# A one-core kernel of two blocks: recurrent merges ahead of the spatial gate, context turns and router shares later, positions added by GpSimd, and three projections in three passes

## What is computed

```python
xn = rms_norm(x, norm_g)
z = xn @ w_in                       # qa ka va fa ga | xb gb | qc kcc ... gc | ud vd gd | mg
y_a = fox_attention(...)            # 8 heads, forgetting attention
y_b = rg_lru(xb, ...)               # recurrent branch
y_c = nsa_attention(...)            # compressed, selected and window attention
u, v = gelu(ud), layer_norm(gelu(vd), ln_v_g)
y_d = u * (einsum('gts,bcsgd->bctgd', w_spatial * causal, v) + b_spatial)
ys = stack([y_a * silu(ga), y_b * silu(gb), y_c * silu(gc), y_d * silu(gd)])
proj = einsum('bsnw,nwd->bsnd', ys, w_branch)          # 4 branches, 512 -> 1024
merged = sum(sigmoid(mg) * proj, axis=branches)
x = x + merged @ w_out
```

## Time and profile before

| | |
|---|---|
| time, median of 3 | 1083.97 us (1081.85 to 1086.04) |
| the profiled execution, its own time | 1090.9 us |
| its span in the trace | 1088.8 us |
| mean granted TensorE clock | 0.955 of full speed |
| TensorE matmul busy | 1007.3 us, 93% |
| VectorE busy | 612.8 us, 56% |
| ScalarE busy | 441.5 us, 41% |
| GpSimd busy | 49.5 us, 5% |

### The profile page before, as it was taken

How to read it: one execution, slowest core, us unless ns; L and a number is a source line. 1 busy time by engine, 2 the same in 40 slices (tenths; PEclk the granted TensorE clock), 3 DMA queues, 4 the chain that set the end, 5 groups by cost and what they waited for, 6 DMA issues and landing times.

```text
span 1088.8 us, 13871 instructions
## 1 busy us (share of the span) xinstructions
PE 1007.3 (93%) x5638; PEld 764.9 (70%) x5638; DVE 612.8 (56%) x1065; ACT 441.5 (41%) x709; POOL 49.5 (5%) x66
## 2 busy tenths in 40 slices
PE   7999989999997998898979999995989999999984
PEld 5688667775896988678967886895965753566521
DVE  4777736563655455326574898666842511597605
ACT  4356532954664443124464101335632300556401
POOL 2000000000000000000010222000000000000010
PEclk8999989999998999899989999997899999999987
DMA  9634676765424744624322134002978997999993
GB/s 302 201 135 148 218 267 232 255 224 206 167 78 155 260 166 155 232 86 156 109 95 92 53 141 155 1 1 68 398 292 303 350 382 284 399 404 404 407 350 142
DMA packets 110413, 230.66 MB, mean 212 GB/s; under 512 B 8300, under 2 KB 15757, under 8 KB 110350
## 3 DMA queue, kind: packets, MB, share of 16 engines
q1 hardware_dynamic: 104144, 216.44, 54.8%
q0 software_dynamic: 2880, 9.71, 2.3%
q10 hardware_dynamic: 3326, 3.63, 1.1%
HBM read 221.11 MB, written 8.65 MB: 211 GB/s over the span
## 4 chain that ended last, share of the span: by engine, by line
PE 75%; DVE 14%; DMA 6%; ACT 3%; issue 2%; ACTq 0%; DVEq 0%
PE bank L791 9%; PE bank L1532 7%; PE bank L1533 7%; PE bank L1534 7%; PE bank L2595 6%; PE bank L756 5%; PE bank L2534 4%; PE bank L2535 4%; PE bank L2536 4%; PE bank L2619 3%; DMA more_slots<-in_moe_w_up 2%; PE bank L1446 2%; PE bank L2527 2%; PE bank L1575 2%; PE bank L967 1%
## 5 line engine op out<-in xcount | busy, mean ns | idle before, releaser
L1532 PE MATMUL bank<-rounded 128*128 128x256 f32 (+1 forms) x656 | 201.8, 308 | 9.0 <-DVE slot_rounded L680 4.3
L1533 PE MATMUL bank<-rounded 128*128 128x256 f32 x592 | 168.4, 284 | 0.0
L1532 PEld LDWEIGHTS bank<-rounded 128*128 128x128 f32 x656 | 126.3, 192 | 21.2 <-issue 9.7
L1534 PE MATMUL bank<-rounded,slot_rounded 128*128 128x256 f32 x472 | 134.8, 286 | 0.0
L791 PE MATMUL bank<-x_and_h,slot 128*128 128x256 f32 x544 | 129.1, 394 | 4.9 <-ACT x_and_h L595 4.9
L791 PEld LDWEIGHTS bank<-x_and_h,slot 128*128 128x128 f32 x544 | 106.1, 198 | 22.4 <-issue 7.7
L1533 PEld LDWEIGHTS bank<-rounded 128*128 128x128 f32 x592 | 113.9, 192 | 1.2 <-issue 1.0
L1522 DVE TENSOR_TENSOR slot_rounded<-slot,rounded 128x1024 fp32r<-128x1024 f32 (+1 forms) x63 | 67.1, 1086 | 68.9 <-ACT rounded L1516 68.7
L1534 PEld LDWEIGHTS bank<-rounded,slot_rounded 128*128 128x128 f32 x472 | 91.3, 193 | 0.0
L839 ACT ACTIVATE arena<-bank 128x256 f32<-128x256 f32 x56 | 21.4, 384 | 118.0 <-PE bank L791 96.3
L1516 ACT ACTIVATE rounded<-slot 128x1024 fp32r<-128x1024 f32 (+1 forms) x63 | 57.7, 943 | 27.0 <-PE bank L1534 23.3
(11 more groups left out here) (493 smaller groups left out, 2067.4 us busy)
## 6 DMA issues: line engine op xcount, KB each, us to landing
slot<-in_w_in SPq DMA_DIRECT2D x26, 2048.0 KB, 8.0
slot<-in_ada_w SPq DMA_DIRECT2D x12, 2048.0 KB, 8.4
slot<-in_moe_w_down SPq DMA_DIRECT2D x11, 2048.0 KB, 16.1
...
```

The source lines that it names most:

```text
L1532: t.do.matmul(dst, w_hi, x_hi, start=start, stop=False)
L1533: t.do.matmul(dst, w_hi, x_lo, start=False, stop=False)
L1534: return t.do.matmul(dst, w_lo, x_hi, start=False, stop=stop)
```

## The change

1. `placed` moves from VectorE to GpSimd, with the same operands and waits; it can run as soon as the positions have landed and h1 is made.
2. `FIRST_PIECES` gets 12 more pieces: gb, ud (4 `channels` each) and vd (4 `pieces`, where there were two `tokens` jobs). They are done in three passes from the h1 of the merges; splits are written two pieces ahead, beginning in gc 2 and gc 3. A weight's first use counts from the job that writes its split. The homes are shared with the query/key tiles, so their splits wait for `head_norm` and `heads` of qc and for the last mixing of forgetting attention.
3. `h1_split` moves from behind `spatial_norm` to behind `cmp_keys`; `spatial_mask` is split off and stands before `cmp_keys`; `spatial_norm` takes one epsilon and one root for both tiles, and Newton steps and scales move to `spatial_scale`, ahead of merge 1 1.
4. In `PLAN` the merges of branch 1 move ahead of gd and `spatial`; `merge_start` 3 stands behind spatial 3. The costs of the fill change (vd counts four `pieces`), so the weave shifts from the first pieces on.
5. The context's turns stand one to five jobs later than their scans; the router's nine share instructions stand behind the one-hot rows 0 and 1.

The core of the diff (`tensor_pieces` takes its parts of h1 from `parts_of_h1` in the same way, and the `pieces` and `channels` functions of ScalarE and VectorE write the split that `piece_beside` names):

```diff
+        SQ0, SQ1 = SQ_HOME, SQ_HOME + NT * W
+        FIRST_HOMES += [Y3, SQ0, SQ1, Y3] + [SQ0, V_HOME, Y3, SQ0] + [V_HOME, Y3, SQ0, V_HOME]
...
-                           ("xb", ("channels", "xb", 3)), ("ud", ("channels", "ud", 3)), ("vd", ("tokens", "vd", 1))):
+                           ("xb", ("channels", "xb", 3)), ("ud", ("channels", "ud", 3)), ("vd", ("pieces", "vd", 3))):
...
+        LATER_FIRST = len(FIRST_PIECES)
+        FIRST_PIECES += [*channels("gb"), *channels("ud"), *in_pieces("vd")]
+
+        def piece_beside(job):
+
+            if job in channels("gc")[2:]:
+                return LATER_FIRST + job[2] - 2
+            p = FIRST_PIECES.index(job) + 2 if job in FIRST_PIECES else len(FIRST_PIECES)
+            return p if p not in (LATER_FIRST, LATER_FIRST + 1) and p < len(FIRST_PIECES) else None
...
-        spatial = [*ud[2:], *tokens("vd"), ("spatial_norm",), *channels("gd"), *[("spatial", j) for j in range(WT)]]
+        spatial = [*ud[2:], *in_pieces("vd"), ("spatial_norm",)]
+        gated = [*channels("gd"), *[("spatial", j) for j in range(WT)]]
         ada = [job for c in range(13) for job in ((("ada", c),) if c < 12 else ()) + ((("ada_turn", c - 1),) if c else ())]
         merge = {n: [("merge", n, dt) for dt in range(KT)] for n in range(4)}
 
-        fill, scored = spread(early + lru + spatial, ada, 10) + merge[1], attention(UNITS)
+        fill, scored = spread(early + lru + spatial, ada, 10) + merge[1] + gated, attention(UNITS)
...
-        PLAN += woven([*channels("cf0"), ("ctx_scan", 0), ("ctx_turn", 0, 0), ("ctx_turn", 0, 1),
-                       *channels("cf1"), ("ctx_scan", 1), ("ctx_turn", 1, 0), ("ctx_turn", 1, 1), *tokens("cv"),
+        PLAN += woven([*channels("cf0"), ("ctx_scan", 0), ("channels", "cf1", 0), ("ctx_turn", 0, 0), ("channels", "cf1", 1),
+                       ("ctx_turn", 0, 1), *channels("cf1")[2:], ("ctx_scan", 1), ("tokens", "cv", 0), ("ctx_turn", 1, 0), ("tokens", "cv", 1), ("ctx_turn", 1, 1),
...
-        PLAN.insert(PLAN.index(("spatial_norm",)) + 1, ("h1_split",))
+        PLAN.insert(PLAN.index(("cmp_keys",)) + 1, ("h1_split",))
         for n in range(4):
-            before = {3: ("merge", 1, KT - 1), 0: ("merge", 3, KT - 1), 2: ("merge", 0, KT - 1)}.get(n, ("merge", n, 0))
+            before = {3: PLAN[PLAN.index(("spatial", WT - 1)) + 1], 0: ("merge", 3, KT - 1), 2: ("merge", 0, KT - 1)}.get(n, ("merge", n, 0))
             PLAN.insert(PLAN.index(before), ("merge_start", n))
+        PLAN.insert(PLAN.index(("cmp_keys",)), ("spatial_mask",))
+        PLAN.insert(PLAN.index(("merge", 1, 1)), ("spatial_scale",))
...
-            for name in names:
+            for name in (*names, *([FIRST_PIECES[piece_beside(job)][1]] if piece_beside(job) else [])):
...
-        @part(VECTOR, "placed")
-        def vector_placed(v):
-            v.wait_ge(*at("position_in"))
-            v.wait_ge(*now("h1"))
-            v.do.tensor_tensor(xT[:, :, :], xT[:, :, :], merged, ALU.add).then_inc(*inc("x_placed"))
+        @part(GPSIMD, "placed")
+        def gpsimd_placed(g):
+            g.wait_ge(*at("position_in"))
+            g.wait_ge(*at("h1", KT - 1))
+            g.do.tensor_tensor(xT[:, :, :], xT[:, :, :], merged, ALU.add).then_inc(*inc("x_placed"))
...
+        def parts_of_h1(p):
+
+            if p < LATER_FIRST:
+                return first_high_of_h1, first_low_of_h1, ("split_first_low", 1)
+            return h1_high, h1_low, ("split_h1_low", 1)
...
-            if p >= 3:
-                a.wait_ge(*at(*FIRST_PIECES[p - 3]))
+            held = [o for o in range(p) if FIRST_HOMES[o] == FIRST_HOMES[p]]
+            if held:
+                a.wait_ge(*at(*FIRST_PIECES[held[-1]]))
             if FIRST_HOMES[p] in (M0, M1):
                 a.wait_ge(*at("x_placed"))
+            if FIRST_HOMES[p] == SQ0:
+                a.wait_ge(*at("head_norm", "done", "qc"))
+            if FIRST_HOMES[p] == SQ1:
+                a.wait_ge(*at("heads", "qc", 1))
+            if p >= LATER_FIRST and FIRST_HOMES[p] == V_HOME:
+                a.wait_ge(*at("mixed", UNITS[2 * WT - 1]))
...
-                high, _, low = first_piece(FIRST_PIECES.index(job))
-                t.wait_ge(*at("split_piece_low", FIRST_PIECES.index(job)))
+                p = FIRST_PIECES.index(job)
+                high, _, low = first_piece(p)
+                h_high, h_low, h_done = parts_of_h1(p)
+                t.wait_ge(*at(*h_done))
+                t.wait_ge(*at("split_piece_low", p))
                 for k in range(KT):
-                    mm = three_passes(t, bank[:, 0:S], high[:, k, :], low[:, k, :], first_high_of_h1[:, k, :], first_low_of_h1[:, k, :], k == 0, k == KT - 1)
+                    mm = three_passes(t, bank[:, 0:S], high[:, k, :], low[:, k, :], h_high[:, k, :], h_low[:, k, :], k == 0, k == KT - 1)
...
+        @part(VECTOR, "spatial_mask")
+        def vector_spatial_mask(v):
+            v.wait_ge(*at("spatial_in"))
+            v.do.tensor_tensor(wsT, wsT, bcast(causal_T, 1, 8), ALU.mult).then_inc(*inc("spatial_norm"))
+
         @part(VECTOR, "spatial_norm")
         def vector_spatial_norm(v):
-            v.wait_ge(*at("spatial_in"))
-            v.do.tensor_tensor(wsT, wsT, bcast(causal_T, 1, 8), ALU.mult).then_inc(*inc("spatial_norm"))
             for tt in range(NT):
                 stats, mv = bn[:, tt, 0:6], bn[:, tt, 6:8]
                 v.wait_ge(*at("tokens_out", "vd", tt))
                 v.do.bn_stats(stats, vd[:, tt, :]).then_inc(*inc("spatial_norm"))
                 v.wait_ge(*now("spatial_norm"))
                 v.do.bn_aggr(mv, stats).then_inc(*inc("spatial_norm"))
-                v.wait_ge(*now("spatial_norm"))
-                v.do.tensor_scalar(bn[:, tt, 8:9], bn[:, tt, 7:8], EPS, None, ALU.add).then_inc(*inc("spatial_norm", "var", tt))
+            v.wait_ge(*now("spatial_norm"))
+            v.do.tensor_scalar(bn[:, :, 8], bn[:, :, 7], EPS, None, ALU.add).then_inc(*inc("spatial_norm", "var"))
+
+        @part(SCALAR, "spatial_norm")
+        def scalar_spatial_norm(a):
+            a.wait_ge(*at("spatial_norm", "var"))
+            scalar_root(a, "spatial_norm", (), bn[:, :, 8], bn[:, :, 9])
+
+        @part(VECTOR, "spatial_scale")
+        def vector_spatial_scale(v):
+            v.wait_ge(*at("root", "spatial_norm"))
+            vector_newton(v, "spatial_norm", bn[:, :, 8], bn[:, :, 9], bn[:, :, 10])
             for tt in range(NT):
-                v.wait_ge(*now("spatial_norm"))
-                v.wait_ge(*at("root", "spatial_norm", tt))
-                vector_newton(v, "spatial_norm", bn[:, tt, 8:9], bn[:, tt, 9:10], bn[:, tt, 10:11])
...
-            for which, oh in enumerate((oh1, oh2)):
-                v.do.tensor_tensor(tmp16, oh, prob, ALU.mult).then_inc(*inc("router_steps"))
-                v.wait_ge(*now("router_steps"))
-                v.do.tensor_reduce(share[:, which], tmp16, AX_X, ALU.add).then_inc(*inc("router_steps"))
-                v.wait_ge(*now("router_steps"))
-            v.do.tensor_tensor(total, share[:, 0], share[:, 1], ALU.add).then_inc(*inc("router_steps"))
-            v.wait_ge(*now("router_steps"))
-            v.do.reciprocal(total, total).then_inc(*inc("router_steps"))
-            v.wait_ge(*now("router_steps"))
-            v.do.tensor_tensor(share, share, bcast(total, 1, 2), ALU.mult).then_inc(*inc("router", "shares"))
...
             onehot(0)
             onehot(1)
+
+
+            for which, oh in enumerate((oh1, oh2)):
+                v.do.tensor_tensor((tmp16, pick)[which], oh, prob, ALU.mult).then_inc(*inc("router_steps"))
+                v.wait_ge(*now("router_steps"))
+                v.do.tensor_reduce(share[:, which], (tmp16, pick)[which], AX_X, ALU.add).then_inc(*inc("router_steps"))
+                v.wait_ge(*now("router_steps"))
+            v.do.tensor_tensor(total, share[:, 0], share[:, 1], ALU.add).then_inc(*inc("router_steps"))
+            v.wait_ge(*now("router_steps"))
+            v.do.reciprocal(total, total).then_inc(*inc("router_steps"))
+            v.wait_ge(*now("router_steps"))
+            v.do.tensor_tensor(share, share, bcast(total, 1, 2), ALU.mult).then_inc(*inc("router", "shares"))
```

40 lines of the change are left out of this document (20 added, 20 removed).

## The result

The changed kernel takes 1075.24 us, median of 6 runs (1072.13 to 1076.46), against 1084.33 us for the kernel before in the same session (6 runs). The ratio is 0.9898 with a 95% interval of 0.9872 to 0.9924: 11 us faster (8 to 14; the medians alone are 9 apart), where 22 had been forecast. The time lies just inside the range (1048 to 1076), the size of the gain does not fit. The profiled execution of the changed kernel took 1076.5 us, 1.2 over its median; that of the kernel before took 1090.9, 6.9 over the median of its first three runs, so the two spans, 1088.8 and 1074.3, are 14.5 apart and overstate the gain. One execution among the experiments, 1983.02 us in experiment one, stood far off in a slow state and is left out of its median and ratio.

A forecast was written before the change was run, and what follows sets the result against it. TensorE's matmul queue, busy 93% of the span, was taken as the bound, so only less matmul work or less waiting helps. Terms sum to -22.2 us from the 1083.97 median: 1062 us, range 1048 to 1076 (eight in ten).

The forecast's parts named there:

- step 1: Early add of positions on GpSimd: VectorE loses 3.8 us, a wait loses 2.3; +1.5 us (-3.0 to +6.0).
- step 2: Weave around compressed attention: three waits and a slow job go, -7.4 us; ada load +1.0, compressed scores' turn +1.2.
- step 5: Spatial's merge after its weights: the load's 5.68 us wait and slowness in the gate go; -8.1 us (0 to -8.1).
- rivals B: Splits in bursts: half of twelve pieces stall 1.5 to 2 us, cancelling three passes' saving; +10, 1072 us, chance 0.27.
- rival C: Slots late: merge 3's load still waits, the gain of step 5 is not had; +8, 1070 us, chance 0.08.
- its own signs of being wrong: Waits: gb, ud or vd splits; merge 3 0, ada or xb loads; or total moving under 10 us with waits gone.
- Step 3: gb, ud and vd in three passes: 7.6 us less TensorE work, one stall of +3.3 us from the splits.
- Step 4: Recurrent merge right behind vd and norm: wait 2.1, slow clock 1.7, about 1.1 for next split; +4.9 us (0 to +7).
- 6, context: Later context turns: waits of 2.35 and 3.81 us and slowness behind each go; -10.0 us (-6.2 to -11).
- 7, router: Nine router share operations leave the chain to the slots; -1.0 us (0 to -1.4).
- Rivals B and D: The second named: every one of twelve pieces stalls 3.3 us, slower than before; 1098 us, chance 0.05.

The follow-up runs named there:

- experiment one: Changed kernel with the add of positions back on VectorE: 1069.92 us (median of 3 runs), ratio to the kernel before 0.988.
- experiments one and two: Changed kernel, first with positions back on VectorE (1069.92 us), second with GpSimd's 128x2048 add cut into eight of 128x256 (1073.63 us).
- the better versions: Changed kernel with positions on VectorE, ada 3 behind xb 0 and further job moves, in three versions: 1065.78, 1062.26 and 1060.17 us.
- Experiment three: Changed kernel with job ada 3 moved back behind xb 0: 1070.7 us (4 runs), ratio to the kernel before 0.9877.
- The four versions of the third stretch: Up to merge 0 0's gate: plain, old order 200.0 us, recurrent merges first 205.7; three passes, old order 201.0, recurrent merges first 195.0 to 198.5.

## Why the prediction was wrong

Three of its steps failed: step 1 priced the add on GpSimd too low, step 2 the load that the new place of ada 3 delays, and step 5 took a load's wait for all that stood there. That the time lies inside the stated range all the same is luck: its upper end was there for rivals B and C, and neither happened. Of its own signs of being wrong two came, a wait behind a split of vd and one for xb's load.

By its own steps, in us; measured is from the table of stretches and the experiments.

| step | forecast | measured |
|---|---|---|
| 1, positions on GpSimd | +1.5 | +5.1 |
| 2, weave around compressed attention | -5.2 | -3.2 |
| 3, work of three passes | -7.6 | -7.2 |
| 3, 4, 5: stall, merge 1 start, merge 3's load | +0.1 | +2.7 to +4.5 |
| 6, context | -10.0 | -10.9 |
| 7, router | -1.0 | -1.1 |
| sum | -22.2 | -14.6 to -12.8; by the ratio -11 (8 to 14) |

The sum of the measured steps is that of traces and lies at the upper edge of what the times say. Between executions with the same code the last stretch alone differs by 8 us (see the last section), more than this gap.

**Step 1** named the right mechanism and took the wrong price. Its own ends were at odds as well: with 6.0 us lost at most and 2.3 gained, the worst case was +3.7, not +6.0. It reasoned from one pair of 128x512 (1.34 us lost) and let the single-operand instructions in VectorE's run count as free. A copy lost 4.5 us to the add, as a two-input product did (4.4). The same section of the Trainium skill that the prediction cites ("SBUF — State Buffer", "Who interferes with whom") says besides that a copy can contend and that a reduction never does; by the rows of experiments one and two the trace agrees with both. So a copy ahead of the ka 2 split was no cover. The later pieces then brought a second wait, idle time of 7.8 us in place of 4.4, and 1.7 us more at the lower clock, which the step did not count at all. (In the three traces in which the add hit the product of 128x1024, the first two waits are one of 6.95 us, with less slow clock behind it and the same length in all.) Going back to VectorE is what the better versions do, and with xb's load out of the way it is worth 6.6 us up to the end of the second stretch (151.90 to 145.33).

**Step 2** had the three waits gone (0.24 left) but priced the new place of ada 3 at +1.0. It made xb's load wait for the slot of cmp_hidden 0: 2.42 us and 1.7 of clock. Experiment three removes the wait with one line. The 1.7 of clock belong to this execution, not to the step: in others nothing was lost there.

**Step 3** held for the work: a gb job is 2.93 us from 229.47 to the next instruction at 232.40, and the stretch's work fell by 7.2. The prediction's other estimate, 10.4 us by the four passes that the Trainium skill states ("FP8 and Floating Point Precision", section "TensorE Precision Notes"), was too much here, as the rows before had shown.

```profile
229.47 0.39 PE L1574 MATMUL bank<-rounded 128*128 128x256 f32 x1
...
232.40 1.03 PE L1005 MATMUL bank<-arena 128*128 128x256 f32 x4
```

Its one stall came as counted, 1.73 us and 1.7 of clock. Rivals B and D did not happen: one of twelve pieces stalls. But the work was all that it gave: the trace of the three passes with the old order (experiment thirteen) takes 201.0 us where plain took 200.0 (195.0 and 196.4 to 197.7 without the time lost to the slow clock).

**Step 4** was about right in idle time (2.36 and 0.64, 3.0 us) and wrong in counting slow clock behind it: TensorE ran at 1.00 after it.

**Step 5** is where most of the rest went. The load no longer waits, as said (so rival C is out), but the step asked only whether the weights would be there, and not who else was late at this place. Before the change ScalarE's part of merge_start 3 ran during the recurrent merges, 10.8 us ahead of its gate:

```profile
327.11 1.05 ACT L1558 ACTIVATE rounded<-arena 128x1024 fp32r<-128x1024 f32 x1
```

Now it begins when spatial ends, 1.2 us behind the start of the gate, and merges 3 0 and 3 1 wait 0.67 and 2.92 us for splits, with 1.4 of clock. Of 8.1 us 5.0 were given back (3.6 in traces where the clock stayed up): the step was worth 3.1 to 4.5, not 8.1.

**Steps 6 and 7** held, with ctx_state late by 0.34 (0.78 before the change).

Last, the sum itself: it added steps 3, 4 and 5 as if independent. The four versions of the third stretch show that they are not. That the context's part, the three passes and the order, each removed alone, cost 11, 10 and 4 us by the ratios (the last not clear of noise) while the whole is worth 11 is the same fact seen from the other end. Why plain projections with the new order are as slow as 205.7 is not settled beyond the waits named: each version has its own weave, and no run changed the order with the weave held.
